# The first norm's gain as one row, spread by TensorE into PSUM

## The chip, the cores and the metric

One core of a Trainium2 chip runs the whole program. The metric is device microseconds of one execution, the median of several runs.

## The reference, cut to what matters

Four layers on 512 tokens of 1024 numbers each. Each layer norms its input, mixes it (attention with a window, a gated mix of chunks, attention over selected keys, then the first kind again), adds the normed result, and does the same with a convolutional feed-forward part. Only the very first norm, and the first attention's bias, are touched by the change:

```python
def rms_norm(x, g):
    xf = x.astype(jnp.float32)
    y = xf * lax.rsqrt(jnp.mean(xf * xf, axis=-1, keepdims=True) + EPS)
    return (y * g.astype(jnp.float32)).astype(x.dtype)
...
    bias = rel_bias[rel_bucket(dist)].astype(jnp.float32)
...
    sc = jnp.einsum('bqkgd,bskd->bkgqs', qb, kb).astype(jnp.float32) * scale + bias
...
    h = rms_norm(x, pre_mix)
```

## The kernel before

The 512 tokens are four tiles of 128 partitions (`TT` is 4, `P` is 128), 1024 columns each (`D`). All products are made of three: every operand is split into a high part in a 32-bit type that TensorE takes at full pace, and a low part, the difference; high by high, high by low and low by high are added up in PSUM. Weights come as slabs of 128x1024 through a ring of four buffers (`raw`): SP loads a slab, ScalarE writes its high part (`split_hi`, L953), VectorE its low part (`split_lo`, L1729), and SP waits for that before it loads the next slab into the buffer (`ring`, L688).

The order on each engine is written out by hand, and semaphores join the engines. At the start of the program it runs like this:

- SP (L676 to L684) issues loads of x tiles one and two, the gain `g_pre`, four weight slabs, x tiles three and four, and the sinks. The gain is one row of 4 KB in HBM, which the DMA writes to all 128 partitions, 512 KB in all.
- GpSimd makes the identity matrices (L777 to L785) and counts in `consts_made`.
- TensorE waits for them and then runs filler matmuls of an identity by itself, which nobody reads (`turn`, L3433): 36, then the two bias matmuls (L3443), which turn the bucket table into 16 rows of 768 bias values in PSUM banks 6 and 7, then 16 more. It then transposes tiles one and two of the normed x (`transposes`, L2732), runs 12 fillers, and starts on the first weights: `first_half` (L2682) does 24 matmuls for the first slab and tiles one and two, in three groups of 8, which wait for the first low half, for the slab's low part and for the second low half; then `forward_columns` (L2699) does the second slab, from L2704.
- ScalarE's order for this first norm is in `norms` (L1060): squares and root of tiles one and two (`root_pre`), the high part of the first slab, a copy of the bias rows from PSUM to SBUF (L1073), the high halves of tiles one and two (`hi`, L1020), three more slabs, then tiles three and four. Behind the first high half it issues the DMA that writes the bias rows to HBM; later DMAs bring them back as a table.
- VectorE's order is in `norms` (L1820): it waits for the gain, then `norm` of tiles one and two (reciprocal, L1763; x times root times gain, L1767), the low part of the first slab, the low halves of both tiles (`lo`, L1772), three more slabs, then tiles three and four.

The order that VectorE follows in the first norm is one tuple:

```python
if k == 0:
    order = (norm, 0), (norm, 1), (split_lo, n), (lo, 0), (lo, 1), (split_lo, n + 1), (split_lo, n + 2), \
            (split_lo, n + 3), (norm, 2), (norm, 3), (lo, 2), (lo, 3)
```

Of the kernel before, what the change touches and what calls it, by code (L numbers as in the profile page):

```python
# [8 lines left out]
P = 128  # L9
D = 1024  # L10
# [70 lines left out]
def build(nc, slabs, x_in, gains, conv, sinks, rel_bias, onehot, wsT, ln_g, ln_b, b_s, kv_g, kidx_g, out):  # L81
# [9 lines left out]
    with ExitStack() as ctx:  # L91
# [580 lines left out]
        def _(sp):  # L672
            def load_x(t):
                sp.dma_start(x[:, t, :], x_in[0, toks(t), :]).then_inc(x_loaded[t], 16)

            load_x(0)  # L676
            load_x(1)
            sp.dma_start(g_pre[:, :], gains[0].partition_broadcast(P)).then_inc(gains_in, 16)
            for r in range(RAW):
                sp.dma_start(raw[:, r, :], slabs[r]).then_inc(raw_in[r], 16)  # L680
            load_x(2)
            load_x(3)
            for s in range(2):
                sp.dma_start(sink_sb[:, s, :], sinks[s].partition_broadcast(P)).then_inc(sinks_in, 16)  # L684

# [90 lines left out]
        def _(pool):  # L776
# [1 line left out]
            pool.memset(ident16[:, :], 0.0).then_inc(consts_made, 1)  # L778
            pool.memset(eps[:, :], EPS).then_inc(consts_made, 1)
            pool.memset(same_tile[:, :], 1.0).then_inc(consts_made, 1)  # L780
            pool.wait_ge(consts_made, 4)
            for m in (ident, ident16):
                pool.affine_select(out=m[:, :], in_=m[:, :], compare_op=ALU.not_equal, fill=1.0, base=0,
                                   pattern=[[-1, P]], channel_multiplier=1).then_inc(consts_made, 1)
# [149 lines left out]
        def _(sc):  # L934
# [125 lines left out]
            def norms(k, n):  # L1060

                root_post, root_pre, hi, last_tile, root_halves = norm_steps(k, n)
                if k == 0:
                    order = (root_pre, 0), (root_pre, 1), (split_hi, n), (hi, 0), (hi, 1), (split_hi, n + 1), \
                            (split_hi, n + 2), (split_hi, n + 3), (root_pre, 2), (root_pre, 3), (hi, 2), (hi, 3)
                else:
                    order = (root_post, 0), (root_pre, 0), (root_post, 1), (hi, 0), (root_pre, 1), \
                            (root_post, 2), (hi, 1), (root_pre, 2), (root_post, 3), (hi, 2), (root_pre, 3), (hi, 3)
                for stage, number in order:
                    stage(number)  # L1070
                    if k == 0 and stage is split_hi and number == n:
                        sc.wait_ge(rows_mm, 1)
                        sc.activation(flat_act[0:HEADS, D:D + 2 * REV].rearrange("p (t c) -> p t c", t=2),  # L1073
                                      ps[0:HEADS, 6:8, 0:REV], ACT.Copy).then_inc(rows_sb, 1)
                    if k == 0 and stage is hi and number == 0:
                        sc.wait_ge(rows_sb, 1)
                        sc.dma_start(bias_rows, flat_act[0:HEADS, D:D + 2 * REV]).then_inc(rows_out, 16)
                    if k == 0 and stage is split_hi and number == n + 3:
                        spread_rows(0)
# [599 lines left out]

            sc.dma_start(rb_sb[:, :], rel_bias).then_inc(rows_in, 16)  # L1680
            sc.dma_start(flat_act[0:BUCKETS, 0:2 * REV], onehot).then_inc(rows_in, 16)
            sc.wait_ge(consts_made, 7)

            sc.activation(rt[:, 15:16], eps[:, 0:1], ACT.Sqrt)
            norms(0, 0)
# [33 lines left out]
        def _(ve):  # L1719
# [17 lines left out]

            def norm_steps(k):
                p0, q0 = TT * (k - 1), TT * k
                if k == 0:  # L1740
                    ve.wait_ge(gains_in, 16)
                else:
                    ve.wait_ge(gains_in, 32 * k + (16 if k < 2 * DEPTH else 0))

                def y(t):

# [14 lines left out]
                def norm(t):  # L1761
                    ve.wait_ge(pre_rt, q0 + t + 1)
                    ve.reciprocal(rinv[:, 4 + t:5 + t], rt[:, 4 + t:5 + t]).then_inc(pre_r, 1)  # L1763
                    if t >= 2:
                        ve.wait_ge(xn_T, q0 + t - 1)
                    ve.wait_ge(pre_r, q0 + t + 1)
                    ve.scalar_tensor_tensor(work[:, 2 + t % 2, :], x[:, t, :], rinv[:, 4 + t:5 + t], g_pre[:, :],  # L1767
                                            ALU.mult, ALU.mult).then_inc(xn_made, 1)

# [43 lines left out]
            def join(L, n):  # L1813
# [3 lines left out]
                ve.wait_ge(h_made, TT * (2 * L + 1) + 2 * (place[1] + 1))  # L1817
                ve.tensor_tensor(whole(*place), hi.bitcast(f32), lo.bitcast(f32), ALU.add).then_inc(in_sum, 1)

            def norms(k, n):  # L1820

                y, add, norm, lo, last_tile, halves = norm_steps(k)
                if k == 0:
                    order = (norm, 0), (norm, 1), (split_lo, n), (lo, 0), (lo, 1), (split_lo, n + 1), (split_lo, n + 2), \
                            (split_lo, n + 3), (norm, 2), (norm, 3), (lo, 2), (lo, 3)
                else:
                    order = (y, 0), (add, 0), (norm, 0), (y, 1), (add, 1), (lo, 0), (norm, 1), \
                            (y, 2), (add, 2), (lo, 1), (norm, 2), (y, 3), (add, 3), (lo, 2), (norm, 3), (lo, 3)
                for stage, t in order:
                    if k % 2 and stage is lo and t == TT - 1:  # L1830
                        join(k // 2, 0)
                        join(k // 2, 3)
                    stage(t)
# [834 lines left out]
        def _(pe):  # L2668
# [127 lines left out]
            def norms_and(k, n, kinds):  # L2796


                def part(g, half):

                    for e in range(2):
                        if k == 0 and g == half == e == 0:
                            first_half(0)
                            continue
                        if g == half == 0:
                            pe.wait_ge(h_made, TT * k + (1 if kinds[0] and e == 0 else 2))
                        if half == 0 and e == 1 and k % 2:
                            transposes(k, 2 + g)
                        if half == 0 and g == 1 and k > 0 and k % 2 == 0:
                            transposes(k, 2 + e)  # L2810
                        if half == 0 and e == 1 and k == 0 and g == 1:
                            transposes(k, 2)
                            transposes(k, 3)
                        need = n + 2 * g + (1 if e or kinds[g] else 0)
                        if half == 0 and n == 0:
                            pe.wait_ge(lo_made, made(need))
                        elif half == 0:
                            pe.wait_ge(early_lo, early_made(need))
                        if kinds[g]:
                            forward_pair_tile(n + 2 * g, 2 * g, 2 * half + e)  # L2820
                        else:
                            forward_half(n + 2 * g + e, 2 * g + e, half)

                if k == 0:
                    transposes(k, 0)
                    transposes(k, 1)
                    turn(12)
                    pe.wait_ge(rows_sb, 1)
                part(0, 0)
                part(1, 0)  # L2830
                pe.wait_ge(h_made, TT * k + 4)
# [598 lines left out]
                        p3(j, 1).then_inc(w_used, 1)  # L3430

            first_pairs = {0: (False, True), 1: (True, True)}
            def turn(times):  # L3433


                for _ in range(times):
                    pe.matmul(ps[:, 5, 0:P], ident16[:, :], ident16[:, :], start=True, stop=True)

            pe.wait_ge(consts_made, 7)
            turn(36)  # L3440
            pe.wait_ge(rows_in, 32)
            for t in range(2):
                last = pe.matmul(ps[0:HEADS, 6 + t, 0:REV], rb_sb[:, :], flat_act[0:BUCKETS, REV * t:REV * (t + 1)],  # L3443
                                 start=True, stop=True)
            last.then_inc(rows_mm, 1)
            turn(16)
            norms_and(0, 0, first_pairs[KINDS[0]])
            for L, kind in enumerate(KINDS):
                n1 = BASE[L] + IN_SLABS[kind]
# [84 lines left out]
```

## Time and profile before

| | |
|---|---|
| runs (us) | 2038.05, 2034.66, 2037.17; median 2037.17 |
| the profiled execution (us) | 2034.89 |
| its span, first to last instruction (us) | 2033.2 |
| granted clock, mean | 1.000 |
| busy: TensorE, VectorE, ScalarE, GpSimd | 99%, 81%, 55%, 20% |
| chain that ended last, by engine | TensorE 86%, VectorE 8%, DMA 3%, ScalarE 1% |

All times in the rows are from the span's start, and the span is that of the profiled execution alone, which is why a sum is made against it. A row of the timeline merges neighbouring instructions of a kind: start, time from the first's start to the last's end, engine, line, operation, and in brackets the idle time ahead of it and what ended it. A matmul's record lasts until its result is out, so neighbouring records overlap, and what a matmul costs in a queue is read from start to start.

### The profile page before, as it was taken

What the parts mean: (1) busy time and instruction counts of PE and PEld (TensorE: products, weight loads), DVE (VectorE), ACT (ScalarE), POOL (GpSimd) and SP (SyncE); (2) the same over time, 40 slices, a digit from 0 to 9 for tenths busy, and PEclk for the clock granted to TensorE, in tenths of its full rate; (3) what the DMA queues carried; (4) which work ended last, traced back from release to release, by engine and by line L of the source; (5) the groups of instructions that cost most, each with busy time, mean ns of one, the idle gap of its engine ahead of it and who ended that gap; (6) DMA issues with size and microseconds to landing.
All of it is one profiled execution on the core that took longest, in us unless ns stands there. A gap on an engine that the chain in (4) does not pass through costs nothing.

```text
span 2033.2 us, 34151 instructions
## 1 busy us (share of the span) xinstructions
PE 2019.5 (99%) x12924; PEld 1757.6 (86%) x12924; DVE 1645.6 (81%) x2629; ACT 1127.1 (55%) x1909; POOL 412.6 (20%) x490
## 2 busy tenths in 40 slices
PE   9999999999999999999999999999999999999998
PEld 8889999888988899888877898998889889999887
DVE  6668889899467888989888668889897668888898
ACT  5755556447325555546656645555465755556455
POOL 1520322210000212311045402123100520222220
PEclk9999999999999999999999999999999999999999
DMA  8133344494431343557421123435674132335393
GB/s 292 64 104 125 120 120 160 130 261 158 146 135 73 94 121 109 182 179 239 162 73 43 63 83 100 127 107 170 193 239 159 64 104 84 119 100 170 116 263 130
DMA packets 83727, 278.58 MB, mean 137 GB/s; under 512 B 9536, under 2 KB 13760, under 8 KB 83184
## 3 DMA queue, kind: packets, MB, share of 16 engines
q1 hardware_dynamic: 59184, 214.67, 31.0%
q0 software_dynamic: 12352, 26.22, 6.5%
q10 hardware_dynamic: 12032, 35.54, 4.7%
q8 instruction: 103, 1.69, 0.3%
q14 instruction: 56, 0.46, 0.1%
HBM read 256.43 MB, written 14.73 MB: 133 GB/s over the span
## 4 chain that ended last, share of the span: by engine, by line
PE 86%; DVE 8%; DMA 3%; ACT 1%; issue 1%; POOL 0%; SPq 0%; DVEq 0%; ACTq 0%; POOLq 0%
PE ps L2676 10%; PE ps L2677 10%; PE ps L2678 10%; PE ps L2888 7%; PE ps L3215 6%; PE ps L3217 6%; PE ps L3216 6%; PE ps L3295 4%; PE ps L3296 4%; PE ps L3297 4%; DMA raw<-slabs 2%; PE ps L2748 2%; PE ps L2704 2%; PE ps L2705 2%; PE ps L2706 2%; DVE w_lo L1729 2%
## 5 line engine op out<-in xcount | busy, mean ns | idle before, releaser
L953 ACT ACTIVATE w_hi<-raw 128x1024 fp32r<-128x1024 f32 x296 | 309.7, 1055 | 152.8 <-DVE raw L2487 71.3
L1729 DVE TENSOR_TENSOR w_lo<-raw,w_hi 128x1024 fp32r<-128x1024 f32 x284 | 357.0, 1265 | 46.0 <-ACT w_hi L953 41.8
L2676 PE MATMUL ps<-h_hi,w_hi 128*128 128x512 f32 (+1 forms) x976 | 383.0, 392 | 0.0
L2677 PE MATMUL ps<-h_lo,w_hi 128*128 128x512 f32 (+1 forms) x976 | 379.6, 389 | 0.0
L2678 PE MATMUL ps<-h_hi,w_lo 128*128 128x512 f32 (+1 forms) x976 | 379.1, 388 | 0.0
L2676 PEld LDWEIGHTS ps<-h_hi,w_hi 128*128 128x128 f32 x976 | 183.4, 188 | 39.2 <-issue 4.0
L2678 PEld LDWEIGHTS ps<-h_hi,w_lo 128*128 128x128 f32 x976 | 183.2, 188 | 38.2
L2677 PEld LDWEIGHTS ps<-h_lo,w_hi 128*128 128x128 f32 x976 | 183.6, 188 | 34.8
L867 POOL TENSOR_TENSOR bias<-act 128x256 f32<-128x256 f32 x40 | 50.2, 1254 | 734.8 <-DVE x_r L2237 429.5
L2164 DVE SCALAR_TENSOR_TENSOR work<-ps,conv_sb,work 128x511 f32<-128x511 f32 (+1 forms) x232 | 169.9, 742 | 25.6 <-ACT work L1349 24.9
L3295 PE MATMUL ps<-w_hi,h_hi 128*128 128x512 f32 x408 | 159.6, 391 | 1.1 <-DVE w_lo L1729 1.1
L3297 PE MATMUL ps<-w_hi,h_lo 128*128 128x512 f32 x408 | 158.8, 389 | 0.0
L3296 PE MATMUL ps<-w_lo,h_hi 128*128 128x512 f32 x408 | 158.8, 389 | 0.0
L1390 ACT ACTIVATE w_hi<-raw 128x1024 fp32r<-128x1024 f32 (+1 forms) x108 | 97.3, 912 | 102.4 <-PE ps L2678 47.5
L1349 ACT ACTIVATE work<-ps,conv_sb 128x512 f32<-128x512 f32 x116 | 88.5, 773 | 88.3 <-PE ps L2678 82.7
L3217 PE MATMUL ps<-h_hi,w_lo 128*128 128x256 f32 x432 | 122.3, 283 | 0.0
L3216 PE MATMUL ps<-h_lo,w_hi 128*128 128x256 f32 x432 | 122.2, 283 | 0.0
L3215 PE MATMUL ps<-h_hi,w_hi 128*128 128x256 f32 x432 | 122.1, 283 | 0.0
L2193 DVE TENSOR_TENSOR w_lo<-raw,w_hi 128x1024 fp32r<-128x1024 f32 (+1 forms) x108 | 113.6, 1052 | 9.5 <-ACT w_hi L1390 9.4
L3295 PEld LDWEIGHTS ps<-w_hi,h_hi 128*128 128x128 f32 x408 | 76.6, 188 | 18.6 <-issue 3.0
L3297 PEld LDWEIGHTS ps<-w_hi,h_lo 128*128 128x128 f32 x408 | 76.6, 188 | 16.0
L3296 PEld LDWEIGHTS ps<-w_lo,h_hi 128*128 128x128 f32 x408 | 76.6, 188 | 15.4
(366 smaller groups left out, 5257.3 us busy)
## 6 DMA issues: line engine op xcount, KB each, us to landing
raw<-slabs SPq DMA_DIRECT2D x368, 512.0 KB, 3.8
act<-slabs POOLq DMA_DIRECT2D x64, 256.0 KB, 5.3
raw<-act POOLq DMA_DIRECT2D x36, 256.0 KB, 3.3
bias<-slabs SPq DMA_DIRECT2D x16, 512.0 KB, 5.8
x_dram<-x ACTq DMA_DIRECT2D x16, 512.0 KB, 4.8
x<-x_dram ACTq DMA_DIRECT2D x16, 512.0 KB, 5.2
act<-slabs SPq DMA_DIRECT2D x12, 512.0 KB, 5.8
bias_dram<-bias_rows ACTq DMA_DIRECT2D x2, 2048.0 KB, 13.7
```

The costliest lines, as they stand in the source:

```text
L953: sc.activation(w_hi[:, c % RING, :], raw[:, raw_slot(c), :], ACT.Copy).then_inc(hi_made, 1)
L1729: ve.tensor_tensor(w_lo[:, c % RING, :], raw[:, raw_slot(c), :], w_hi[:, c % RING, :].bitcast(f32), ALU.subtract).then_inc(lo_made, 1)
L2164: ve.scalar_tensor_tensor(y, ps[:, up_bank(q, e), 0:SEQ - sh], scale, y, ALU.mult, ALU.add).then_inc(done, 1)
L2676: pe.matmul(ps[:, bank, cols], hi, h_hi[:, k, cols], start=k == 0, stop=False)
L2677: pe.matmul(ps[:, bank, cols], hi, h_lo[:, k, cols], start=False, stop=False)
L2678: last = pe.matmul(ps[:, bank, cols], lo, h_hi[:, k, cols], start=False, stop=k == KT - 1)
L3215: pe.matmul(o, hi[:, w], b_hi[:, k, :], start=begin and k == 0, stop=False, skip_group_check=onto)
L3216: pe.matmul(o, hi[:, w], b_lo[:, k, :], start=False, stop=False, skip_group_check=onto)
L3217: last = pe.matmul(o, lo[:, w], b_hi[:, k, :], start=False, stop=k == KT // 2 - 1, skip_group_check=onto)
L3295: pe.matmul(ps[:, bank, :], hi[at], w_hi[:, s, cols], start=begin, stop=False, skip_group_check=onto)
L3296: pe.matmul(ps[:, bank, :], hi[at], w_lo[:, s, cols], start=False, stop=False, skip_group_check=onto)
L3297: return pe.matmul(ps[:, bank, :], lo[at], w_hi[:, s, cols], start=False, stop=end, skip_group_check=onto)
```

## The change

SP loads the gain first as one row of 4 KB, into row 0 of a work buffer. TensorE multiplies it by a row of ones that GpSimd has set, in two matmuls of 512 columns, so that banks 4 and 5 of PSUM hold the gain in all 128 partitions. VectorE's norms of tiles one and two read it there. The 512 KB form is loaded later, behind the x tiles, for tiles three and four, and SP waits for the two matmuls before it issues it. The filler matmuls become 16, 8 and 8, in bank 3. The copy of the bias rows goes from ScalarE to VectorE, which does it between the second norm and the first low half; TensorE's wait for that copy moves from the first weights to the transposes of tile four, which write the banks. On VectorE the split of the first slab moves from ahead of the first low half to behind it.

```diff
+            sp.dma_start(work[0:1, 0, :], gains[0].partition_broadcast(1)).then_inc(gains_in, 16)
             load_x(0)
             load_x(1)
-            sp.dma_start(g_pre[:, :], gains[0].partition_broadcast(P)).then_inc(gains_in, 16)
...
             load_x(3)
+            sp.wait_ge(rows_mm, 1)
+            sp.dma_start(g_pre[:, :], gains[0].partition_broadcast(P)).then_inc(gains_in, 16)
...
+            pool.memset(work[0:1, 3, 0:P], 1.0).then_inc(consts_made, 1)
-            pool.wait_ge(consts_made, 4)
+            pool.wait_ge(consts_made, 5)
...
-                    if k == 0 and stage is split_hi and number == n:
-                        sc.wait_ge(rows_mm, 1)
-                        sc.activation(flat_act[0:HEADS, D:D + 2 * REV].rearrange("p (t c) -> p t c", t=2),
-                                      ps[0:HEADS, 6:8, 0:REV], ACT.Copy).then_inc(rows_sb, 1)
...
-                if k == 0:
-                    ve.wait_ge(gains_in, 16)
-                else:
-                    ve.wait_ge(gains_in, 32 * k + (16 if k < 2 * DEPTH else 0))
+                if k > 0:
+                    ve.wait_ge(gains_in, 16 + 32 * k + (16 if k < 2 * DEPTH else 0))
...
                     ve.wait_ge(pre_r, q0 + t + 1)
+                    if k == 0 and t < 2:
+                        ve.wait_ge(rows_mm, 1)
+                        ve.scalar_tensor_tensor(two(work[:, 2 + t, :]), two(x[:, t, :]), rinv[:, 4 + t:5 + t],
+                                                ps[:, 4:6, :], ALU.mult, ALU.mult).then_inc(xn_made, 1)
+                        return
+                    if k == 0:
+                        ve.wait_ge(gains_in, 32)
...
+            def keep_rows(t):
+
+                ve.wait_ge(rows_mm, 2)
+                ve.tensor_copy(flat_act[0:HEADS, D:D + 2 * REV].rearrange("p (t c) -> p t c", t=2),
+                               ps[0:HEADS, 6:8, 0:REV]).then_inc(rows_sb, 1)
...
-                    order = (norm, 0), (norm, 1), (split_lo, n), (lo, 0), (lo, 1), (split_lo, n + 1), (split_lo, n + 2), \
+                    order = (norm, 0), (norm, 1), (keep_rows, 0), (lo, 0), (split_lo, n), (lo, 1), (split_lo, n + 1), (split_lo, n + 2), \
...
                             transposes(k, 2)
+                            pe.wait_ge(rows_sb, 1)
                             transposes(k, 3)
...
-                    turn(12)
-                    pe.wait_ge(rows_sb, 1)
+                    turn(12, 5)
...
-            pe.wait_ge(consts_made, 7)
-            turn(36)
+            def spread_gain():
+
+                pe.wait_ge(gains_in, 16)
+                for half in range(2):
+                    last = pe.matmul(ps[:, 4 + half, :], work[0:1, 3, 0:P], work[0:1, 0, half * SEQ:(half + 1) * SEQ],
+                                     start=True, stop=True)
+                last.then_inc(rows_mm, 1)
+
+            pe.wait_ge(consts_made, 8)
+            turn(16, 3)
+            spread_gain()
+            turn(8, 3)
             pe.wait_ge(rows_in, 32)
...
             last.then_inc(rows_mm, 1)
-            turn(16)
+            turn(8, 3)
             norms_and(0, 0, first_pairs[KINDS[0]])
```

TensorE's queue from the program's start to the first weights, before (`ident` is the identity, so `ps<-ident` are the fillers, `ps<-act,rb_sb` the bias matmuls, `ps<-ident,work` the transposes):

```order
L3437 MATMUL ps<-ident 128x128 [waits consts_made]
L3437 MATMUL ps<-ident 128x128 x35
L3443 MATMUL ps<-act,rb_sb 16x384 [waits rows_in]
L3443 MATMUL ps<-act,rb_sb 16x384
L3437 MATMUL ps<-ident 128x128 x16
L2736 MATMUL ps<-ident,work 128x128 [waits xn_made]
...
L2691 MATMUL ps<-h_hi,w_hi 128x256 [waits h_made,h_hi_made,hi_made,rows_sb]
```

and the same stretch after the change:

```order
L3446 MATMUL ps<-ident 128x128 [waits consts_made]
L3446 MATMUL ps<-ident 128x128 x15
L3452 MATMUL ps<-work 128x512 [waits gains_in]
L3452 MATMUL ps<-work 128x512
L3446 MATMUL ps<-ident 128x128 x8
L3462 MATMUL ps<-act,rb_sb 16x384 [waits rows_in]
L3462 MATMUL ps<-act,rb_sb 16x384
L3446 MATMUL ps<-ident 128x128 x8
L2746 MATMUL ps<-ident,work 128x128 [waits xn_made]
...
L2701 MATMUL ps<-h_hi,w_hi 128x256 [waits h_hi_made,h_made,hi_made]
```

Ahead of the transposes 20 fillers are gone and the two spreading matmuls (`ps<-work`) have come in, with a wait for the row; the first weights no longer wait for the bias copy.

VectorE's queue over the first two norms and the low halves, before:

```order
L1763 RECIPROCAL rinv<-rt 128x1 [waits pre_rt,gains_in]
L1767 SCALAR_TENSOR_TENSOR work<-x,rinv,g_pre 128x1024 [waits pre_r]
L1763 RECIPROCAL rinv<-rt 128x1 [waits pre_rt]
L1767 SCALAR_TENSOR_TENSOR work<-x,rinv,g_pre 128x1024 [waits pre_r]
L1729 TENSOR_TENSOR w_lo<-raw,w_hi 128x1024 [waits hi_made]
L1772 TENSOR_TENSOR h_lo<-ps,h_hi 128x8x128 [waits h_hi_made] x2
L1729 TENSOR_TENSOR w_lo<-raw,w_hi 128x1024 [waits hi_made] x3
```

and after the change:

```order
L1760 RECIPROCAL rinv<-rt 128x1 [waits pre_rt]
L1766 SCALAR_TENSOR_TENSOR work<-x,rinv,ps 128x1024 [waits rows_mm,pre_r]
L1760 RECIPROCAL rinv<-rt 128x1 [waits pre_rt]
L1766 SCALAR_TENSOR_TENSOR work<-x,rinv,ps 128x1024 [waits rows_mm,pre_r]
L1827 COPY act<-ps 16x768 [waits rows_mm]
L1776 TENSOR_TENSOR h_lo<-ps,h_hi 128x8x128 [waits h_hi_made]
L1728 TENSOR_TENSOR w_lo<-raw,w_hi 128x1024 [waits hi_made]
L1776 TENSOR_TENSOR h_lo<-ps,h_hi 128x8x128 [waits h_hi_made]
L1728 TENSOR_TENSOR w_lo<-raw,w_hi 128x1024 [waits hi_made] x3
```

The norms wait for the spreading matmuls (`rows_mm`) where they waited for the DMA, the bias copy has come in ahead of the low halves, and the first slab's split stands between them.

## Rows read from the trace of the kernel before

**Rows 1.** The page's first part: busy time, share of the span, instructions.

```profile
PE 2019.5 (99%) x12924; PEld 1757.6 (86%) x12924; DVE 1645.6 (81%) x2629; ACT 1127.1 (55%) x1909; POOL 412.6 (20%) x490
```

**Rows 2.** The chain of waits, 0 to 60 us: start, us, what.

```profile
1.75 6.05 DMA g_pre<-gains
...
8.02 1.28 DVE work L1767
9.42 1.28 DVE work L1767
...
11.84 1.19 DVE h_lo L1772
```

**Rows 3.** The timeline of TensorE, 0 to 24 us.

```profile
2.42 4.02 PE L3437 MATMUL ps<-ident 128*128 128x128 bf16 x36 [2.42 <-POOL same_tile L785]
6.37 1.79 PE L3443 MATMUL ps<-act,rb_sb 32*16 32x384 f32 x4
8.10 1.07 PE L3437 MATMUL ps<-ident 128*128 128x128 bf16 x16
9.37 1.09 PE L2736 MATMUL ps<-ident,work 128*128 128x128 f32 x8 [0.20 <-DVE work L1767]
...
13.28 1.19 PE L2691 MATMUL ps<-h_hi,w_hi 128*128 128x256 f32 x8 [0.76 <-DVE h_lo L1772]
...
16.23 0.28 PE L2704 MATMUL ps<-h_hi,w_hi 128*128 128x256 f32 x1
...
21.99 1.91 PE L2736 MATMUL ps<-ident,work 128*128 128x128 f32 x16
```

**Rows 4.** The timeline of TensorE, 7.4 to 7.8 and 7.8 to 8.2 us.

```profile
6.99 1.17 PE L3443 MATMUL ps<-act,rb_sb 32*16 32x384 f32 x3
...
7.36 0.80 PE L3443 MATMUL ps<-act,rb_sb 32*16 32x384 f32 x2
```

**Rows 5.** 2.4 to 6.4 us: busy PE, PEld, DVE, ACT, POOL; granted clock, DMA, GB/s.

```profile
2.40:6.40 4.00, 3.98 (x37) 3.79 (x38) 0.00 (x0) 2.28 (x5) 0.00 (x0) 1.00 0.99 349
```

**Rows 6.** DMA issues, 0 to 14 us: KB each, us from issue to landing.

```profile
act<-onehot ACTq DMA_DIRECT2D x1, 96.0 KB, 4.7
...
rb_sb<-rel_bias ACTq DMA_DIRECT2D x1, 2.0 KB, 3.2
```

**Rows 7.** The timeline of SP's queue and of GpSimd, 0 to 2 us.

```profile
0.83 0.87 SPq L674 DMA_DIRECT2D x<-x_in  x2
...
1.10 0.10 POOL L779 MEMSET eps<- 128x1 f32 x1
```

**Rows 8.** The timeline of ScalarE, 4 to 12 us.

```profile
4.78 1.06 ACT L996 ACTIVATE work<-x 128x1024 f32<-128x1024 f32 x1 [1.53 <-DMA x<-x_in]
...
6.56 1.06 ACT L996 ACTIVATE work<-x 128x1024 f32<-128x1024 f32 x1 [0.30 <-DMA x<-x_in]
...
7.74 0.30 ACT L999 ACTIVATE rt<-ss,eps 128x1 f32<-128x1 f32 x1
...
10.07 0.78 ACT L1073 ACTIVATE act<-ps 16x768 f32<-16x768 f32 x1
10.76 1.00 ACT L1020 ACTIVATE h_hi<-ps 128x1024 fp32r<-128x1024 f32 x1
```

**Rows 9.** VectorE by line and shape: count | busy us, mean ns | idle before.

```profile
L1754 DVE SCALAR_TENSOR_TENSOR work<-ps,rinv,g_post 128x1024 f32<-128x1024 f32 x29 | 37.2, 1284 | 2.7
...
L1989 DVE COPY act<-ps 64x512 f32<-64x512 f32 x16 | 11.0, 689 | 6.9 <-PE ps L2706 6.7
...
L1993 DVE COPY vbuf<-ps 128x1024 f32<-128x1024 f32 x2 | 2.5, 1225 | 0.6 <-PE ps L2722 0.5
```

**Rows 10.** The timeline of VectorE, 10 to 46 us.

```profile
10.62 1.22 DVE L1729 TENSOR_TENSOR w_lo<-raw,w_hi 128x1024 fp32r<-128x1024 f32 x1
...
19.82 1.28 DVE L1767 SCALAR_TENSOR_TENSOR work<-x,rinv,g_pre 128x1024 f32<-128x1024 f32 x1
...
45.98 0.43 DVE L1950 COPY_PREDICATED ps<-same_tile,ps 128x256 f32<-128x256 int32 x1 [2.25 <-PE ps L3010]
```

More of the change, by code:

```diff
@@ L1681, in _ @@
             sc.dma_start(flat_act[0:BUCKETS, 0:2 * REV], onehot).then_inc(rows_in, 16)
-            sc.wait_ge(consts_made, 7)
+            sc.wait_ge(consts_made, 8)
             sc.activation(rt[:, 15:16], eps[:, 0:1], ACT.Sqrt)
@@ L3432, in _, with turn @@
             first_pairs = {0: (False, True), 1: (True, True)}
-            def turn(times):
+            def turn(times, bank):
                 for _ in range(times):
-                    pe.matmul(ps[:, 5, 0:P], ident16[:, :], ident16[:, :], start=True, stop=True)
-            pe.wait_ge(consts_made, 7)
-            turn(36)
+                    pe.matmul(ps[:, bank, 0:P], ident16[:, :], ident16[:, :], start=True, stop=True)
+            def spread_gain():
[8 more added lines that the diff above has]
+            turn(8, 3)
             pe.wait_ge(rows_in, 32)
```

## The prediction

> **What bounds the kernel now.** First the busy times: TensorE is busy for 99% of the span [rows 1], so the program as a whole is a line of matmuls, and a change at its start is worth what it moves the first matmul on real weights. The span is 2033.2 us, the profiled execution took 2034.89 us, and the three runs have a median of 2037.17 us.
>
> So I read the chain of waits of the first 60 us next [rows 2]. It begins with the DMA that spreads the gain over the partitions: issued at 1.75 us, it takes 6.05 us. VectorE then does the first two norms (8.02 and 9.42, 1.28 us each), one weight split, and the low half of tile one at 11.84, after which TensorE starts on weights. Seen from this chain, removing that DMA is worth 1.5 us: the root of tile one is there at about 6.3 (its squares began at 4.78, and tile two's root ends 1.48 after its squares began [rows 8]), and VectorE begins when the DMA is there, 1.75 + 6.05 = 7.80.
>
> The third view, TensorE's timeline [rows 3], says something else. Its queue before the first transposes is full: 36 filler matmuls from 2.42 (4.02 us), the two bias matmuls from 6.37, 16 fillers from 8.10 that last to 9.17. The transposes of tile one start at 9.37, 0.20 us after VectorE let them. TensorE itself would not have been free before about 9.0. A norm that is ready earlier finds TensorE busy. That is what the rest turns on.
>
> The clock matters here. The granted clock reads 1.00 from 2.40 to 6.40 [rows 5], as if at the upper level of 2.4 GHz. But 36 matmuls of 128 columns in 4.02 us are 0.11 us each, which is the lower level, 1.2 GHz. The bias matmuls show the rise: each is issued as two pieces, so there are four of 384 columns. The first, at 6.37, lasts until the next at 6.99 (0.62 us); the last two, from 7.36, are through when the fillers start at 8.10 (0.37 us each, issue included) [rows 3, 4]. So the clock rose about 7.0 to 7.4, some 4.7 us after TensorE began.
>
> **The change, part by part.**
>
> *The row and the loads.* The one-row DMA goes ahead of both x loads on SP. Two x issues take 0.87 us [rows 7], so x moves back by 0.44. For landing the nearest row is the 2 KB of bias weights, 3.2 us from issue; the bound above is the 96 KB one-hot, 4.7 us [rows 6]. I take 3.2, since 4 KB is nearest to it: there at 0.83 + 3.2 = 4.0, at most 5.5. The squares of tile one move from 4.78 to 5.2, of tile two from 6.56 to 7.0, the second root from 7.74 to 8.2 and ends at 8.5 [rows 8].
>
> *The memset.* One more on GpSimd; a small one shows 0.10 us [rows 7], and its queue is what TensorE starts on: 2.42 becomes 2.5.
>
> *The spreading matmuls.* They are not in the trace. Like the bias matmuls they are 32-bit, two matmuls, hence four pieces, of 512 columns: 0.62 x 512/384 = 0.83 us a piece at the lower level, half of that, 0.42, at the upper. Bounds: 1.7 to 3.3 us. Behind 16 fillers (16 x 0.11) they start at 4.3. Three pieces at the lower level end at 6.8, the fourth straddles the rise and ends at about 7.4; with the way out, VectorE may read at 7.5.
>
> *TensorE's queue behind it.* Of 52 fillers 32 are left, so 20 go, but the spreading is 4 x 512 pieces more and falls in the slow part. After 7.4: 8 fillers at half of 0.11 (0.45), four bias pieces at 0.37 (1.47), 8 fillers (0.45): free at 9.75. The transposes of tile one start at 9.75 instead of 9.37 and end after 1.09 at 10.84 [rows 3]. They now wait for TensorE, not for VectorE.
>
> *VectorE.* Norm one starts at 7.55 instead of 8.02; reading a PSUM operand costs the same (1284 ns with one [rows 9], 1.28 us without [rows 2]). Norm two starts at 8.95 instead of 9.42 and ends at 10.2. The bias copy, 16x768, lies between 64x512 at 0.69 and 128x1024 at 1.23 [rows 9]; by columns 0.96, so it ends at 11.2. It is free of cost as long as the first high half is later than that, and it is.
>
> *ScalarE.* It loses the copy of 0.78 us at 10.07. In the trace the high half of tile one started at 10.76, when that copy was through, though its transposes were done at 10.46 [rows 3, 8]. Now it starts at 10.9, bound by TensorE: later by 0.15. The low half follows, at 12.0 instead of 11.84, and ends at 13.2.
>
> *The new order on VectorE.* Before, the split of the first weight slab stood ahead of the low half of tile one, and there it was covered by waiting for ScalarE. Now it stands between the two low halves. After the end of the first low half (11.84 + 1.19 = 13.03) TensorE had 24 matmuls to do and began the next slab, line L2704, at 16.23, 3.2 us later and paced by itself [rows 2, 3]. Now VectorE has the split (1.22), the second low half (1.19) and the next split (1.22) to do in that stretch [rows 2, 10]: 3.63, and 0.22 for the handing over (13.03 to 13.28 shows 0.25). That is 3.85 us: TensorE waits 0.65 more.
>
> *What is hidden.* The third and fourth tiles: their transposes start at 21.99 with no idle time ahead of them, and the fourth norm was through at 21.10 [rows 3, 10]; the copy's later DMA and the full gain's later load eat into that 0.9, and TensorE is later too. If that cover were gone, each 0.1 would be 0.1 on the end. The bias table: at 45.98 VectorE waits for a matmul, not for the table [rows 10]. The next slab loads are issued 2.4 us later, since the first split is; ScalarE wants them only after the first products.
>
> **Sum:** +0.15 and +0.65, so +0.8 us at L2704, carried to the end because TensorE is busy from there on. Against the profiled execution that is 2035.7 us. The median of the runs is 2.3 us above that execution, and the middle of all four times is 2036.0; 2037.17 + 0.8 and 2036.0 + 0.8 give 2038.0 and 2036.8. I take **2037.4 us**: no change that can be told, as 0.2% is 4.1 us, about what a measurement of this kernel can tell from none.
>
> The moment of the rise is the softest number. "TensorE: Matmul & The Clock Gate" in the Trainium skill (section What you observe) has the rise come about half a microsecond earlier or later from run to run; the trace here holds one rise only and cannot say. By that page the queue would be free a quarter of a microsecond earlier or later, and the sum between +0.55 and +1.05 instead of +0.8.
>
> **The rivals.**
>
> *The gain comes through (chance 0.13).* If the clock rises a microsecond earlier, or x lands as early as before, norm one starts at 6.95 and TensorE is free at about 8.3. Then the transposes end at 9.4, the high half at 10.5, the low half follows the bias copy and ends at 11.8, and L2704 starts at 15.65: -0.6 us. For it: the gain's 512 KB no longer run between x and the weights. Against it: x is issued later, and the new order costs its 0.65 in any case. That puts the time at 2036.0, still no change by the bound.
>
> *The clock rises late (0.09).* The spreading matmuls have one row of weights instead of 128 and stand where TensorE was doing full fillers when the clock rose; a wait for a row that lands at 5.5 would add a pause ahead of them. If the lower level held until the transposes, the queue would run 2.5 + 3.5 + 3.3 + 2.5 = 11.8 instead of 9.75: +2.05, in all +2.8 us and 2040.0. The bias matmuls, 32 by 16, ran while the clock rose and after [rows 4], which speaks against it.
>
> *The clock stays low (0.03), the side of slower.* The same mechanism, but the lower level lasts into the weights' matmuls. The first 8 transposes (0.12 each) and the first 48 matmuls (0.12 each) would take twice as long: +1.0 and +5.8 on top of +2.05, some +8 us less the 0.65 then covered, 2045. It decides once more than about 15 of these matmuls run at the lower level.
>
> **How the numbers follow.** The forecast, +0.8 give or take 0.7, has the other 0.75. The range goes from the lowest run less 0.6 (2034.1) to the highest plus 2.8 (2040.8); I give 2034.0 to 2040.8. Faster by over 0.2% (below 2033.1) needs something that none of the cases holds: 0.02. Slower by over 0.2% (above 2041.2) is the third rival and an odd run: 0.04. Within: 0.94.
>
> **What would show it.** In the profile after: norm one on VectorE at about 7.5, waiting for TensorE and no longer for a DMA; the transposes of tile one starting at 9.75 right behind fillers; the high half at about 10.9 with no copy ahead of it; a wait of TensorE for VectorE's split ahead of L2704, near 17.0. I am wrong on the step if the spreading takes 1.7 us (the clock is up before it), wrong on the order if TensorE has no idle time between its first weight matmul and L2704, and wrong as a whole if the first layer's matmuls start more than 2 us away from where they did.

## The result, and the profile after

The changed kernel takes 2039.38 us (median of 22 runs, 2037.65 to 2041.41), the kernel before 2036.22 us (22 runs in the same rounds, 2034.53 to 2038.62). The ratio is 1.0015, with a 95% interval of 1.0009 to 1.0020: 1.8 to 4.1 us slower, less than the 0.2% that counted as a change, and inside the range that was given. The forecast of 2037.4 us and +0.8 us was nevertheless wrong in its main step, as TensorE's timeline shows at once. Its columns are those of [rows 3]: start, duration, engine and line, operation, idle time ahead.

```profile
2.55 1.89 PE L3446 MATMUL ps<-ident 128*128 128x128 bf16 x16 [2.55 <-POOL same_tile L788]
4.37 3.78 PE L3452 MATMUL ps<-work 1*128 1x512 f32 x4
8.08 1.03 PE L3446 MATMUL ps<-ident 128*128 128x128 bf16 x8
9.04 2.74 PE L3462 MATMUL ps<-act,rb_sb 32*16 32x384 f32 x4
11.71 1.03 PE L3446 MATMUL ps<-ident 128*128 128x128 bf16 x8
12.54 3.52 PE L2746 MATMUL ps<-ident,work 128*128 128x128 f32 x16
15.89 0.83 PE L3446 MATMUL ps<-ident 128*128 128x128 bf16 x12
17.26 1.18 PE L2701 MATMUL ps<-h_hi,w_hi 128*128 128x256 f32 x8 [0.54 <-ACT h_hi L1023]
...
20.31 0.36 PE L2714 MATMUL ps<-h_hi,w_hi 128*128 128x256 f32 x1
```

TensorE is never idle from 2.55 us until the transposes of both tiles are through, and everything in that stretch runs at the pace of the lower level, 1.2 GHz. From start to start a filler takes 0.12 us (8 in 9.04 - 8.08), a piece of the spreading 0.93 us ((8.08 - 4.37)/4), a bias piece 0.67 us ((11.71 - 9.04)/4), a transpose 0.21 us ((15.89 - 12.54)/16). Before, the bias pieces ended at 0.37 us and the transposes took 0.12 us [rows 3, 4]. The 12 fillers from 15.89 us, through in 0.83 us, are the first at the upper level, 2.4 GHz. So the clock rose at about 15.7 us instead of 7.0 to 7.4 us. The second slab's matmuls (L2714 here, L2704 before) start at 20.31 us instead of 16.23 us, 4.08 us later.

The granted clock column does not tell this. A window of TensorE in the same execution (stretch, its length, busy time and count, granted clock, DMA share, GB/s) reads 1.00 while the pace is half:

```profile
8.10:12.50 4.40, 4.40 (x21) 1.00 1.03 412
```

VectorE's timeline and ScalarE's, the counterparts of [rows 8, 10]:

```profile
8.27 1.28 DVE L1766 SCALAR_TENSOR_TENSOR work<-x,rinv,ps 128x1024 f32<-128x1024 f32 x1 [0.90 <-PE ps L3452]
...
9.66 1.28 DVE L1766 SCALAR_TENSOR_TENSOR work<-x,rinv,ps 128x1024 f32<-128x1024 f32 x1
11.82 0.95 DVE L1827 COPY act<-ps 16x768 f32<-16x768 f32 x1 [0.88 <-PE ps L3462]
15.54 1.23 DVE L1776 TENSOR_TENSOR h_lo<-ps,h_hi 128x1024 fp32r<-128x1024 f32 x1 [2.78 <-ACT h_hi L1023]
16.69 1.22 DVE L1728 TENSOR_TENSOR w_lo<-raw,w_hi 128x1024 fp32r<-128x1024 f32 x1
```

```profile
5.69 1.06 ACT L999 ACTIVATE work<-x 128x1024 f32<-128x1024 f32 x1 [2.46 <-DMA x<-x_in]
...
14.49 1.02 ACT L1023 ACTIVATE h_hi<-ps 128x1024 fp32r<-128x1024 f32 x1 [5.01 <-PE ps L2746]
16.09 1.02 ACT L1023 ACTIVATE h_hi<-ps 128x1024 fp32r<-128x1024 f32 x1 [0.58 <-PE ps L2746]
```

The DMA that spread the gain is gone from the path: norm one waits for the spreading matmuls. But the norms were not what the transposes waited for. Norm two is through at 9.66 + 1.28 = 10.94 us, the transposes start at 12.54 us without idle time, ScalarE stands 5.01 us waiting for TensorE, and VectorE 2.78 us waiting for ScalarE. The chain of waits says the same; its part up to the first weights (start, length, engine, line) no longer holds a DMA, and is TensorE's queue up to one high half on ScalarE (the fillers and bias matmuls between are left out here):

```profile
4.44 3.71 PE ps L3452 x4
...
12.74 3.33 PE ps L2746 x16
16.09 1.03 ACT h_hi L1023
17.26 1.18 PE ps L2701 x8
```

What the start costs can be read further down, at VectorE's norm behind the first layer's mix. The first of these rows is from VectorE's timeline before, the second after:

```profile
141.09 1.28 DVE L1754 SCALAR_TENSOR_TENSOR work<-ps,rinv,g_post 128x1024 f32<-128x1024 f32 x1
```

```profile
145.20 1.28 DVE L1751 SCALAR_TENSOR_TENSOR work<-ps,rinv,g_post 128x1024 f32<-128x1024 f32 x1
```

It is 4.11 us later: the whole delay, carried on unchanged. I call this difference the shift at 141 us, and the experiments are read by it, because it is finer than the time. Two profiled executions of the kernel before (one was run again, below) differ there by 0.03 us and at the end by 2.9 us, which arises in the feed-forward parts, where the change does nothing.

### The profile page after: what moved, and what is told of

The parts are those of the page before. It is cut to its first block, busy times and chain, and to the rows that moved or that the text cites. A ratio compares the mean times of both kernels' runs of the same rounds, so it can differ in the third digit from the quotient of the medians.

```text
span 2036.9 us, 34122 instructions
## 1 busy us (share of the span) xinstructions
PE 2024.0 (99%) x12908; PEld 1758.7 (86%) x12908; DVE 1644.1 (81%) x2630; ACT 1125.2 (55%) x1908; POOL 415.6 (20%) x491
## 3 DMA queue, kind: packets, MB, share of 16 engines
q8 instruction: 103, 1.69, 0.3%
## 4 chain that ended last, share of the span: by engine, by line
PE 89%; DVE 7%; DMA 2%; ACT 1%; issue 1%; POOL 0%; SPq 0%; DVEq 0%; ACTq 0%; POOLq 0%
PE ps L2686 10%; PE ps L2687 10%; PE ps L2688 10%; PE ps L2898 7%; PE ps L3225 6%; PE ps L3227 6%; PE ps L3226 6%; PE ps L3305 5%; PE ps L3306 5%; PE ps L3307 5%; PE ps L2758 2%; PE ps L2714 2%; PE ps L2715 2%; PE ps L2716 2%; DMA raw<-slabs 1%; PE ps L2746 1%
```

## The experiments

Two theories were to be told apart. **A:** the clock rises late because matmuls with few rows of weights, the spreading above all, have taken the place of full fillers. **B:** it has nothing to do with the rows: more columns stand in the queue, x and the row land later, and the order on VectorE costs its share.

| kernel | transposes start, us for one | second slab starts | shift at 141 us | ratio to before (95%) |
|---|---|---|---|---|
| before | 9.37, 0.12 | 16.23 | 0 | 1 |
| the change | 12.54, 0.21 | 20.31 | +4.11 | 1.0015 (1.0009 to 1.0020) |
| change, 128 rows | 10.70, 0.11 | 17.60 | +1.42 | 1.0011 (1.0002 to 1.0020) |
| change, 128 rows, no late start | 9.63, 0.11 | 16.54 | +0.36 | 1.0000 (0.9990 to 1.0010) |
| before, with one-row matmuls | 12.96, 0.20 | 20.50 | +4.26 | 1.0026 (1.0016 to 1.0037) |
| before, with 128-row matmuls | 10.79, 0.11 | 17.36 | +1.10 | 1.0003 (0.9993 to 1.0012) |
| before, with 32-by-16 matmuls | 12.66, 0.21 | 20.40 | +4.16 | 1.0018 (1.0008 to 1.0027) |
| change, fillers first | 9.40, 0.19 | 17.23 | +1.04 | 1.0015 (1.0006 to 1.0024) |
| change, 16-bit spreading | 9.80, 0.19 | 17.57 | +1.38 | 0.9998 (0.9988 to 1.0007) |
| change, old order | 12.54, 0.21 | 20.31 | +4.03 | 1.0017 (1.0008 to 1.0026) |
| before, bias matmuls behind | 9.40, 0.12 | 16.98 | +2.25 | 1.0004 (0.9995 to 1.0013) |
| change, repaired | 10.29, 0.12 | 17.88 | +1.69 | 1.0017 (1.0008 to 1.0026) |

**The spreading with 128 rows.** The same columns at the same place, but the whole identity as weights:

```diff
-                    last = pe.matmul(ps[:, 4 + half, :], work[0:1, 3, 0:P], work[0:1, 0, half * SEQ:(half + 1) * SEQ],
+                    last = pe.matmul(ps[:, 4 + half, :], ident[:, :], vbuf[:, 0, half * SEQ:(half + 1) * SEQ],
```

> The spreading matmuls keep their 2 x 512 columns but take 128 rows (the identity by a block of ones) instead of one; the gain's row is still waited for, and tiles one and two are normed without their gain. Theory A (the one-row matmuls leave TensorE at the lower clock through the transposes): the fillers and bias matmuls behind the spreading run at the upper level, from about 7 to 8 us; the transposes of tile one start near 9.8 instead of 12.5, and the time is about 0.8 us above before (2037.0 against 2036.2). Theory B (the added columns, the later x loads and VectorE's order cost it at any clock): transposes still after 12, about 3 us above before.

The clock rose in the spreading's last piece and the transposes ran at 0.11 us; of the 4.11 us, 2.69 were gone. But VectorE's memset of the operand had held up GpSimd, and TensorE began at 3.09 us instead of 2.55 us. So it was run again with only the spreading waiting for the memset.

> As the first experiment (spreading 128 rows deep, tiles one and two without their gain), but TensorE's start no longer waits for the block of ones. Theory A: fillers from 2.5, rise during the spreading, transposes from 9.8 to 10.2 at the upper level, second slab from 17.0: 0.8 us behind before's 16.23, which is the sum on record. Theory B: 3 us behind.

TensorE's timeline of this run:

```profile
2.55 1.89 PE L3447 MATMUL ps<-ident 128*128 128x128 bf16 x16 [2.55 <-POOL same_tile L788]
4.23 3.18 PE L3454 MATMUL ps<-vbuf,ident 128*128 128x512 f32 x4
7.25 0.61 PE L3447 MATMUL ps<-ident 128*128 128x128 bf16 x8
7.79 1.46 PE L3464 MATMUL ps<-act,rb_sb 32*16 32x384 f32 x4
9.18 0.62 PE L3447 MATMUL ps<-ident 128*128 128x128 bf16 x8
9.63 1.92 PE L2747 MATMUL ps<-ident,work 128*128 128x128 f32 x16
...
13.10 1.19 PE L2702 MATMUL ps<-h_hi,w_hi 128*128 128x256 f32 x8 [0.88 <-DVE h_lo L1777]
...
16.54 0.35 PE L2715 MATMUL ps<-h_hi,w_hi 128*128 128x256 f32 x1
```

The spreading's last piece and all that follows are at the upper level (a bias piece in (9.18 - 7.79)/4 = 0.35 us). This is the queue that the prediction drew. It is the change without its effect on the clock, and it costs 0.36 us at 141 us, and nothing that the time shows. Theory B is left with a tenth of the delay.

**The other way round: few rows in the kernel before.** No row, no PSUM operand, no new order; 20 of the first 36 fillers give way to two matmuls of 512 columns that nobody reads.

```diff
-            turn(36)
+            turn(16)
+            for half in range(2):
+                pe.matmul(ps[:, 4, :], vbuf[0:1, 1, 0:P], vbuf[0:1, 0, half * SEQ:(half + 1) * SEQ], start=True, stop=True)
```

> The kernel before, with the last 20 of the first 36 fillers replaced by two matmuls with one row of weights and 2 x 512 columns, whose result nobody reads. Theory A: the clock is still at the lower level when the 16 fillers run; these end near 12, the transposes of tile one start near 12 instead of 9.4, and the time is 2.5 to 4 us above before. Theory B: the added columns alone, at the clock that before had, move the transposes by some 0.5 us, and the time by at most 0.8.

The control has `ident[:, :], vbuf[:, 0, ...]` in that line, which is 128 rows deep:

> The control for the second experiment: the kernel before with the same two added matmuls of 2 x 512 columns in place of 20 fillers and the same later start, but 128 rows deep. Theory A: rise during these matmuls, transposes near 10.3 at the upper level, the time at least 2.5 us below that of the one-row form and 1 us above before. Theory B: the same as the one-row form, 4 to 5 us above before.

and a third one `ps[0:16, 4, :], vbuf[0:32, 1, 0:16], vbuf[0:32, 0, ...]`, the shape of the bias matmuls:

> The kernel before with 20 of its 36 fillers replaced by two matmuls of 512 columns, as in the runs with one row and with 128 rows, but of 32 rows by 16 columns of weights, the shape of the bias matmuls; the columns and the start (3.08 us) stay the same. If any few rows of weights keep TensorE at the lower level, bias-shaped ones do too: transposes of tile one at about 13.0 us at 0.20 us apiece, the second slab at about 20.5, the first layer's norm 4.2 us later than before. If only the single row does it, the clock rises in this stretch as with 128 rows: transposes at about 10.8 at 0.11 apiece, second slab 17.4, the norm 1.1 us later. In between (as 1.5 to 3 us later) would say that the number of rows matters by degrees.

TensorE's timeline with one row, with 128 rows, and with 32 by 16:

```profile
4.90 3.78 PE L3444 MATMUL ps<-vbuf 1*128 1x512 f32 x4
8.61 2.74 PE L3447 MATMUL ps<-act,rb_sb 32*16 32x384 f32 x4
...
12.96 3.38 PE L2738 MATMUL ps<-ident,work 128*128 128x128 f32 x16
```

```profile
4.77 3.73 PE L3444 MATMUL ps<-vbuf,ident 128*128 128x512 f32 x4
8.43 1.52 PE L3447 MATMUL ps<-act,rb_sb 32*16 32x384 f32 x4
...
10.79 1.92 PE L2738 MATMUL ps<-ident,work 128*128 128x128 f32 x16
```

```profile
4.90 3.59 PE L3444 MATMUL ps<-vbuf 32*16 32x512 f32 x4
8.29 2.76 PE L3447 MATMUL ps<-act,rb_sb 32*16 32x384 f32 x4
...
12.66 3.59 PE L2738 MATMUL ps<-ident,work 128*128 128x128 f32 x16
```

All three start at 3.08 or 3.09 us, 0.66 us later than the kernel before. Without anything else of the change the one-row matmuls cost 3.16 us more than their control (+4.26 against +1.10 us), and those in the shape of the bias matmuls 3.06 us more (+4.16 us). So it is not something about a single row, and at 32 rows there is no sign of a half effect. Whether the rows alone count, or how many weights a matmul has in all, is not separated: no run has 32 rows by 128 columns of weights.

**Fillers first.** `turn(32, 3)` ahead of the spreading, none behind it, so that the clock is up before the few rows come.

> The changed kernel with its 32 fillers all ahead of the spreading matmuls instead of 16, 8 and 8 around them: the same work in TensorE's queue. Theory A: the fillers run until 6.0, the clock rises near 7 as before, the spreading ends near 8.2, the transposes start near 9.8, and the time is about 1 us above before. Theory B: as the changed kernel, 3 us above before.

The rise came among the fillers, at about 5.2 us (32 of them in 3.16 us, 2.55 to 5.71), and the spreading took 0.48 us a piece. Then the clock fell, the one time that the granted clock column shows a lower level (TensorE's windows, columns as above):

```profile
7.60:8.40 0.80, 0.80 (x4) 1.00 1.03 410
8.40:8.80 0.40, 0.40 (x3) 0.84 1.11 440
8.80:9.20 0.40, 0.40 (x1) 0.50 0.95 379
9.60:11.60 2.00, 2.00 (x11) 0.50 1.01 401
12.40:14.00 1.60, 1.06 (x16) 1.00 1.03 410
```

The 0.84 of the second window puts the fall at about 8.7 us. What ran before it were the one-row pieces from 5.71 us and the bias pieces from 7.62 us. So few rows not only put the rise off, they also let a raised clock go, in this one run; the bias pieces alone, 1.4 us of them with 128 rows in the spreading, did not. The shift of +1.04 us is a quarter of the change's. The time does not show it: its ratio stands for 3 us, from runs between 2034.64 and 2041.20 us, and I leave that open.

**A short stretch of few rows.** The spreading as 16-bit matmuls, one pass instead of two (the gain is then cut to its upper 16 bits):

```diff
-                    last = pe.matmul(ps[:, 4 + half, :], work[0:1, 3, 0:P], work[0:1, 0, half * SEQ:(half + 1) * SEQ],
+                    last = pe.matmul(ps[:, 4 + half, :], work[0:1, 3, 0:P].bitcast(bf16)[:, 1:2 * P:2],
+                                     work[0:1, 0, half * SEQ:(half + 1) * SEQ].bitcast(bf16)[:, 1:2 * SEQ:2],
```

> The changed kernel with the spreading cut to a quarter: the upper halves of the row's numbers are read as 16-bit numbers, so tiles one and two are normed with a gain cut to 16 bits. The stretch with one row of weights shrinks from 3.7 us to 0.9 at the lower level. Theory A, if its length is what counts: the clock rises before or during the bias matmuls, the transposes start at 9.5 or earlier at the upper level, and the front is within 0.7 us of before. Theory A, if any such stretch there puts the rise off: the transposes still run at 0.21 us apiece, from about 9.4, and the front is 2 us late. Theory B (columns): the front is within 0.7 us of before, whatever the clock does.

```profile
4.38 1.03 PE L3452 MATMUL ps<-work 1*128 1x512 bf16 x2
...
6.30 2.74 PE L3463 MATMUL ps<-act,rb_sb 32*16 32x384 f32 x4
...
9.80 3.21 PE L2746 MATMUL ps<-ident,work 128*128 128x128 f32 x16
12.84 0.83 PE L3446 MATMUL ps<-ident 128*128 128x128 bf16 x12
```

The spreading shrinks to 0.96 us (5.34 - 4.38), and yet TensorE's timeline has the bias pieces and the transposes at the lower level, and the rise at about 12.4 us, among the last transposes. The 2.7 us gained at 141 us are the shorter queue and three microseconds of earlier rise. In the kernel before, the same bias pieces began 0.07 us later, and the clock rose among them [rows 4]; here 0.96 us of fillers less stood ahead of them.

**The old order on VectorE.** The split ahead of the first low half again.

> The changed kernel with VectorE's split of the first slab back ahead of the first low half. Theory A: the low halves wait for ScalarE's high halves, which come after 15, so the order is free: the same as the changed kernel within 0.3 us, and no idle time goes from TensorE's first weights. Theory B (the step on record, 0.65 us for the new order): 0.65 us faster than the changed kernel, near 2.5 us above before.

Little difference (+4.03 against +4.11 us): in the change the first weights wait for the second high half, which comes late at the lower level, and that covers most of what the order costs. The comparison is not clean, since the clock rose later in this execution, at about 17.2 us: nearly all of the 12 fillers behind the transposes ran at the lower level, while the change did the same 12 in 0.83 us.

```profile
15.95 1.46 PE L3446 MATMUL ps<-ident 128*128 128x128 bf16 x12
```

What the order costs is read better on TensorE, from the first matmul on weights to the second slab: 2.95 us before (13.28 to 16.23 [rows 3]), 2.94 us here (17.37 to 20.31), 3.05 us in the change (17.26 to 20.31). So the new order cost the change 0.1 us.

**The bias matmuls behind the transposes, in the kernel before.** 64 fillers, the bias matmuls at the place of `turn(12)`, the copy behind the second high half.

> The kernel before with its bias matmuls taken from between the fillers to behind the transposes of tiles one and two (in place of 12 fillers), 64 fillers in one piece ahead, the ScalarE copy of the bias rows behind the second high half, and TensorE's wait for it ahead of the transposes of tile four. Theory A: the clock rises near 7 and the transposes start at 9.3 as before; a single median within 0.5 us of before if before's clock never fell, and 0.5 to 1.5 us below it, with a narrower spread, if part of before's runs lose time to small matmuls. Theory B: no change, within 0.5 us; the bias table comes 3 us later, with 3.3 us to spare.

No gain: the transposes start at 9.40 us against 9.37, after a wait of 0.87 us for norm one, so the kernel before loses nothing there by its own bias matmuls. The run shows what a hidden piece costs once its cover is gone. TensorE's timeline at the transposes of tiles three and four, which started without idle time before [rows 3]:

```profile
23.54 1.09 PE L2736 MATMUL ps<-ident,work 128*128 128x128 f32 x8 [0.57 <-DVE work L1767]
25.09 1.06 PE L2736 MATMUL ps<-ident,work 128*128 128x128 f32 x8 [0.46 <-DVE work L1767]
```

The second slab starts 0.75 us late (a wait of 0.64 us for its low part), then 1.03 us for norms three and four. The other half microsecond of the shift of +2.25 us is not traced.

**A repaired change.** The row in a block of 128 rows that is zero elsewhere, loaded over ScalarE's queue; 24 fillers on either side; the bias matmuls behind the transposes; the old order and the copy on ScalarE.

> The change without what theory A holds against it: the gain's row lies in a block of 128 rows whose others are zero, so that the spreading is 128 rows deep; 24 fillers ahead of it and 24 behind, the bias matmuls behind the transposes as in e6, the row issued on ScalarE's queue so that x is not moved back, VectorE's order as before and the bias copy on ScalarE. Theory A: spreading from about 5.1, over at 7.9 to 8.4, norm one within 0.4 us of before's 8.02, transposes near 9.4: the same as e6 within 0.7 us, and at least 2 us faster than the changed kernel. Theory B (columns and loads): 2 us or more above before.

The clock is up for the spreading (0.45 us a piece) and the transposes, as theory A has it. It rose between the last of the 24 fillers and the spreading, so this run does not show that rows of zeros bring it up. But on that queue the row was there only at 6.85 us, and the spreading waited for it:

```profile
6.85 1.98 PE L3457 MATMUL ps<-work 128*128 128x512 f32 x4 [0.88 <-DMA work<-gains]
```

+1.69 us, no better than the kernel before, and the expected 2 us over the change are not in the time. Its ratio stands for 3.5 us, more than the shift; with the fillers first it is the second run where time and shift disagree by two microseconds.

**The same kernels once more, one run each.**

> The kernel before, unchanged, for a second look at when its clock rises. Theory A as it now stands (small matmuls, the one-row ones and the 32x16 bias ones, do not keep the clock up or bring it up; the fillers and the weights' matmuls do): the bias matmuls and the 16 fillers behind them run at the upper level again, or, if the rise comes later than 7.4 in this execution, the transposes start later than 9.4 and the first weights later than 13.3 by the same amount.

> The changed kernel, unchanged, for a second look. Theory A: transposes of tile one near 12.5 at 0.21 us apiece, the rise near 15.7, the first weights near 17.3, as in the first look.

Before, again, TensorE's timeline:

```profile
2.41 3.58 PE L3437 MATMUL ps<-ident 128*128 128x128 bf16 x36 [2.41 <-POOL same_tile L785]
5.97 1.46 PE L3443 MATMUL ps<-act,rb_sb 32*16 32x384 f32 x4
...
9.37 1.09 PE L2736 MATMUL ps<-ident,work 128*128 128x128 f32 x8 [0.94 <-DVE work L1767]
```

All four bias pieces ran at the upper level (0.35 us each, 5.97 to 7.36), and the 36 fillers took 3.56 us instead of 3.95: the rise came among the fillers, at about 5.4 us, some 1.6 us earlier than in the first execution. It gained nothing, because TensorE then waited 0.94 us for norm one; the first weights came at 13.28 us as before, the shift is -0.03 us, the time 2031.97 us.

The change, again: the first nine transposes at the lower level, the rest at the upper, the rise at about 14.6 us, 1.1 us earlier than in the first execution, and yet the shift is +4.12 us, the time 2040.38 us. TensorE's timeline:

```profile
16.88 1.18 PE L2701 MATMUL ps<-h_hi,w_hi 128*128 128x256 f32 x8 [0.75 <-DVE h_lo L1776]
...
20.32 0.36 PE L2714 MATMUL ps<-h_hi,w_hi 128*128 128x256 f32 x1
```

The weights start 0.38 us earlier, but the second slab starts when it did: 3.44 us behind them, 0.49 more than before. Here VectorE's new order takes back what the earlier rise gives. The late rise is the change's own and not one odd execution: with the old order's run, three executions with this queue on TensorE had it at 14.6, 15.7 and 17.2 us.

## Why the prediction was right and wrong

The time came out within 0.2% and within the range, but the case that was called likeliest did not happen. The second rival did, "the clock rises late", which had a chance of 0.09 and a time of 2040.0 us. That the time lies in the range is not the mechanism's doing: the range was drawn up to 2040.8 us, wide enough for this rival.

- **The step that failed:** "the fourth straddles the rise and ends at about 7.4". The moment of the rise was taken from the kernel before, as if it hung on when TensorE began. It hangs on what TensorE runs: with 128 rows in the same place it came at about 6.8 us, with one row at 15.7 us. It also moves by itself. "A norm that is ready earlier finds TensorE busy", on which the rest was to turn, holds for the first execution of the kernel before and not for the second, where the rise came at 5.4 us and TensorE waited 0.94 us for norm one.
- **The row, the memset, x.** The row landed in time (no idle time ahead of the spreading at 4.37 us); the fillers began at 2.55 us against 2.5. The squares moved by 0.91 us (4.78 to 5.69) against 0.44, at no cost: norm one waited 0.90 us longer for the spreading.
- **The spreading.** 0.93 us a piece at the lower level against 0.83, all four there; done at 8.08 us against 7.4, norm one at 8.27 us against 7.55.
- **The queue behind it.** 0.67 us a bias piece against 0.37, the fillers 0.12 us against 0.06; transposes at 12.54 us against 9.75. They took 0.21 us each, and the first high half came at 14.49 us against 10.9.
- **The new order** was to cost 0.65 us. In the first execution of the change it cost 0.1 us (20.31 against 17.26 + 2.95 = 20.21), because the wait for the second high half covered the rest; in the second, with the earlier rise, about 0.3 us, counted as in the forecast from the end of the first low half (16.79 to 20.32, 3.53 us against 3.2). TensorE's rows show no idle time between its first weights and the second slab, the sign that the prediction had named against this step, but a matmul's record covers such a short wait: the loss is there from start to start. Where the clock is up it costs about half of the forecast: with 128 rows and no late start the first low half ends at 11.77 + 1.23 = 13.00 us and the second slab starts at 16.54, 3.54 us later, against 3.2 before and 3.85 forecast. That is 0.34 us, and the shift of that run +0.36. Given the clock, the sum +0.8 was 0.4 too large: the +0.15 did not come either, with the transposes at 9.63 us and the first high half at 10.72, against 10.76 before.
- **The copy on VectorE** took 0.95 us against 0.96, a norm with its gain in PSUM 1.28 us as said. **What was called hidden** stayed hidden: the transposes of tiles three and four start at 26.14 us without idle time.
- **The rival.** Its price, +2.8 us, is within the measured interval of 1.8 to 4.1, though at 141 us the shift is 4.11: it let the clock rise ahead of the transposes, which in fact cost another 16 x 0.09 = 1.4 us, and it counted the order's 0.65, which was then mostly covered. Its time of 2040.0 us is +2.8 on another base than the forecast's (2037.4 - 0.8 = 2036.6), on which it would have been 2039.4. The argument against it, "the bias matmuls, 32 by 16, ran while the clock rose and after", was misread. It shows that few rows don't stop a rise when 36 full fillers stand ahead of them, not that they may take the place of the fillers. In the kernel before, those 36 are what brings the clock up (in its second execution it rose among them), and the change took 20 of them away.
- **The third rival**, the lower level into the weights, was missed by little: the rise came 1.5 us ahead of the first matmul on weights, and with the old order 0.2 us.

"TensorE: Matmul & The Clock Gate" in the Trainium skill (section What you observe) has the rise move by about half a microsecond from run to run. The runs here do not agree: it moved by some 1.6 us between the two executions of the kernel before (7.0 to 7.4 and 5.4 us) and by 2.6 us between the three with the change's queue (14.6, 15.7 and 17.2 us). And no allowance from run to run was the right one for a change in the work itself, which moved it by 7 us and more.

## What to carry to other kernels

Fillers ahead of the first real work are part of that work's time: before replacing any of them, ask whether what takes their place fills TensorE's rows. A broadcast by a one-row matmul costs its own columns and, at the start of a program, the clock of all that follows until full matmuls have run for a while; it wants a place where the clock is kept up by others, or 128 rows of weights, as in the runs with the identity. That padding one row with zeros does as well is not shown: in the one run that did it the clock was up already. And take the pace from durations start to start, since the granted clock can read 1.00 at half pace, and a short wait between matmuls does not show as idle time.

## What was not expected of the hardware

- TensorE ran matmuls without a gap from 2.55 to 15.7 us at the lower level, where 128-row matmuls of the same columns had the clock up in their last pieces or just behind them, 6.8 to 8.5 us from the span's start in three runs. In the kernel before, with 1 by 128 and with 32 by 16 weights in that place, the rise came at about 16 us.
- A raised clock fell at about 8.7 us behind 3.0 us of such matmuls, though TensorE was busy all the time, and was back at about 12.1 us (one run).
- With full fillers from the start, the rise still came at 5.4 us in one execution of the kernel before and at 7.0 to 7.4 in the other.
- The granted clock reads 1.00 up to the first rise, at half pace, and 0.50 only in the one run with a fall.
- A row of 4 KB ahead of x on SP's queue moved its issue by 0.41 us (0.83 to 1.24) and the first squares by 0.91 us (from 4.78 us; 5.60 to 6.36 in seven executions with the row there); over ScalarE's queue, behind the x loads, the same row took 4.66 us from issue to use (2.19 to 6.85).

Open stay the runs where time and shift differ by some 2 us, each near the edge of its interval (fillers first and repaired are slower than their shift, the 16-bit spreading is faster), whether rows alone or all the weights of a matmul count, and how many full matmuls must stand among small ones for the clock to rise, which was not tried.
